# Gate projections inside the attention stages: plain float32 products replaced by split products whose weights are copied between softmax units

## The reference, cut to what matters

```
gates = jax.nn.sigmoid(gate_logits.reshape(B, S, N_BRANCH, D))   # gate_logits = u @ w_in[..., gates]
merged = gates[:, :, 0] * y_mla + gates[:, :, 1] * y_hg + gates[:, :, 2] * y_mem
x = x + merged @ w_out[l]
```

## Time and profile before

| | |
|---|---|
| time, median of 3 runs | 3338.9 us (3335.42 to 3340.44) |
| span of the profiled execution | 3341.3 us |
| TensorE busy | 91% of the span |
| VectorE busy | 48% |
| ScalarE busy | 41% |
| mean granted TensorE clock | 0.947 of full speed |
| bytes read from HBM | 467 MB, 142 GB/s over the span |

### The profile page before, as it was taken

One profiled execution on the slowest core, in us unless ns is written; L12 is line 12 of the kernel. 1 busy time (PEld: TensorE's weight loads), 2 busy tenths in 40 slices (PEclk: granted clock), 3 DMA queues, 4 the chain that ended last, 5 costly groups with the idle time before them and its releaser, 6 DMA issues.

```text
span 3341.3 us, 51733 instructions
## 1 busy us (share of the span) xinstructions
PE 3024.7 (91%) x21202; PEld 2815.0 (84%) x21202; DVE 1608.4 (48%) x2590; ACT 1374.4 (41%) x1959; POOL 6.5 (0%) x10
## 2 busy tenths in 40 slices
PE   5988979899998889999799898999989988899997
PEld 5988768898998778899799886779979988677996
DVE  5556522454555743255555334445555532444555
ACT  4435442243444434243443345534344332553433
POOL 0000000000000000000000000000000000000000
PEclk9999989999999999999899888999989988899998
DMA  5653354565664244366466542346546555224663
GB/s 157 177 156 117 115 139 126 150 179 163 173 167 143 82 126 126 124 170 172 134 181 176 174 115 76 86 130 187 163 144 179 165 149 128 76 77 126 187 169 114
DMA packets 767009, 475.89 MB, mean 142 GB/s; under 512 B 66640, under 2 KB 750192, under 8 KB 766704
## 3 DMA queue, kind: packets, MB, share of 16 engines
q1 hardware_dynamic: 763408, 462.86, 49.0%
q0 software_dynamic: 3424, 10.49, 1.2%
HBM read 467.01 MB, written 6.29 MB: 142 GB/s over the span
## 4 chain that ended last, share of the span: by engine, by line
PE 71%; DVE 11%; DMA 9%; ACT 7%; issue 1%; SPq 0%; DVEq 0%; ACTq 0%
PE ps L740 31%; PE ps L814 31%; PE ps L831 6%; DVE WL L1473 5%; DMA RING<-in_w_ffn_out 4%; ACT WH L1185 3%; DMA RING<-in_w_in 3%; DMA RING<-in_ffn_wo 2%; PE ps L907 2%; DVE U L1447 1%; PE ps L883 1%; PE ps L771 1%; ACT L1182 1%; ACT REGION L1265 0%; DVE U L1455 0%
## 5 line engine op out<-in xcount | busy, mean ns | idle before, releaser
L1185 ACT ACTIVATE WH<-RING 128x2048 fp32r<-128x2048 f32 (+1 forms) x374 | 645.4, 1726 | 1072.0 <-PE ps L814 389.6
L1473 DVE TENSOR_TENSOR WL<-RING,WH 128x2048 fp32r<-128x2048 f32 (+1 forms) x374 | 769.5, 2057 | 617.8 <-ACT WH L1185 617.0
L814 PE MATMUL ps<-UH,WH 128*128 128x256 f32 x2816 | 415.2, 291 | 29.1 <-ACT UH L1203 29.1
L740 PE MATMUL ps<-REGION,RING 128*128 128x256 f32 (+3 forms) x1904 | 396.4, 370 | 29.9 <-DVE REGION L1932 13.1
L831 PE MATMUL ps<-HH,WH 128*128 128x256 f32 x1408 | 400.1, 284 | 19.3 <-DVE WL L1473 19.1
L740 PEld LDWEIGHTS ps<-REGION,RING 128*128 128x128 f32 (+2 forms) x1904 | 338.8, 190 | 86.0 <-DVE REGION L1932 14.8
L814 PE MATMUL ps<-UH,WL 128*128 128x256 f32 x2816 | 403.2, 287 | 8.2 <-DVE WL L1473 8.2
L814 PEld LDWEIGHTS ps<-UH,WH 128*128 128x128 f32 x2816 | 376.5, 196 | 38.7 <-issue 33.1
L814 PE MATMUL ps<-UL,WH 128*128 128x256 f32 x2816 | 401.0, 286 | 0.0
L831 PE MATMUL ps<-HL,WH 128*128 128x256 f32 x1408 | 397.2, 282 | 0.0
L831 PE MATMUL ps<-HH,WL 128*128 128x256 f32 x1408 | 397.0, 282 | 0.0
(11 more groups left out here) (207 smaller groups left out, 2962.6 us busy)
## 6 DMA issues: line engine op xcount, KB each, us to landing
RING<-in_w_ffn_in SPq DMA_DIRECT2D x176, 512.0 KB, 5.0
RING<-in_ffn_wi SPq DMA_DIRECT2D x176, 512.0 KB, 5.0
RING<-in_w_in SPq DMA_DIRECT2D x86, 1024.0 KB, 5.3
RING<-in_w_ffn_out SPq DMA_DIRECT2D x64, 704.0 KB, 4.8
RING<-in_ffn_wo SPq DMA_DIRECT2D x64, 704.0 KB, 4.7
RING<-in_w_out SPq DMA_DIRECT2D x16, 1024.0 KB, 5.2
RING<-in_w_in SPq DMA_DIRECT2D x48, 256.0 KB, 4.6
RING<-in_w_mem_kv SPq DMA_DIRECT2D x8, 1024.0 KB, 5.1
```

The lines of the kernel that those rows point to most:

```text
L740: last = nc.tensor.matmul(o, a, b, start=i == 0, stop=i == len(terms) - 1)
L814: last = nc.tensor.matmul(bank(n, 0, T), a[:, k, side * P:(side + 1) * P], b[:, k, :], start=i == 0 and k == 0, stop=i == 2 and k == DK - 1)
L1185: nc.scalar.activation(part(WH, s), RING[:, s % SLOTS, 0:pl.words[s]], ACT.Copy).then_inc(weights_high, 1)
L1473: v_.tensor_tensor(part(WL, s), RING[:, s % SLOTS, 0:pl.words[s]], part(WH, s).bitcast(FP), ALU.subtract)\
```

## The change

The gate slabs of the five attentions become split slabs. ScalarE and VectorE take them up between units, each at the head of its iteration i, at the slab that `gate_slab` names. TensorE waits for the low part and runs 24 products a tile in place of the plain product.

```diff
@@ def attention(name, kind): in make_plan
-            pl.slab(f[m * ATTN[kind][0] // DK] + m % (DK // ATTN[kind][0]))
+            pl.slab(f[m * ATTN[kind][0] // DK] + m % (DK // ATTN[kind][0]), split=True)
@@ new, beside class Feed
+        def gate_slab(name, kind, i):
+
+            units = ATTN[kind][0]
+            return slab_first[name] + min((i + units // DK) * (DK // units) // 2, 3)
@@ attention, TensorE
-                            wait_weights(pe, sl)
+                            wait_split(pe, sl)
                             product(f[i] + j, [(bank(f[i] + j, 0, T),
-                                                [(slot(sl, DK, 256)[:, k, m % 2 * P:(m % 2 + 1) * P], U[:, k, :]) for k in range(DK)])])
+                                                feature(parts(sl, DK, 256), UP, DK, slice(m % 2 * P, (m % 2 + 1) * P)))])
@@ attention, ScalarE
                     if i < units:
+                        feed.to(gate_slab(name, kind, i))
                         qt = par = i % 2
                         act.wait_ge(max_ready, base + i + 1)
```

## The result

| | before | changed |
|---|---|---|
| time, median of 4 runs on one chip | 3338.7 us (3335.4 to 3340.4) | 3361.7 us (3360.8 to 3368.8) |
| ratio to before | 1 | 1.0072, 95% interval 1.006 to 1.0085 |
| span of the profiled execution | 3341.3 us | 3359.4 us |
| mean granted TensorE clock | 0.947 | 0.938 |

The change costs 23 us, 0.7%; 16.4 were forecast.

A forecast was written before the change was run, and what follows sets the result against it. TensorE, busy 91% of the span, was taken to bound the kernel. Gains of 0.54 us a tile against added loops, starts and clock losses summed to +16.4 us on 3338.9: 3355 us, own range 3346 to 3364, whole range 3334 to 3368.

The forecast's parts named there:

- The clean pair of `A`: Two steady units of A with one slab: 11.25 us against 9.35 before, +1.9 a pair.
- ScalarE's floor: ScalarE's own work in two loaded units: 10.3 us in A, 10.6 in mla, only a little below the loop.
- The starts: Each attention stage's start: slab 0's subtraction delays T(0) by 1.5 us in mla and C, 3.0 A, 2.3 B, 1.9 mem.
- `mem`'s first unit lost its clock: Start of mem: TensorE's idle grows from 2.21 to 4.1 us and slows its clock, +1.9 us for each mem.
- `mla` of 1.0: This stage: slabs 2 and 3, slowed by the bias_rows write, land near 461 and 476; +1.3 us, bounds -18 and +12.
- the rival that gave 3366: In mla of 1.0, slab 2 still lands at 474 and blocks ScalarE in iteration 3: +12 for +1.3; chance 0.12.
- The rival "no change": In mla of 1.0, slabs issued earlier land in time, the 18 us stall goes; about 3336 us; chance 0.12.
- the 16.4 of the sum: All ten attention stages: two A +9.8, two B +3.6, two C and mla of 1.1 +2.7, two mem -1.0, mla of 1.0 +1.3.
- its last sentence: Signs of error: pairs under 9.35 us, a granted clock drop in steady pairs, or the write letting slabs through.
- a loaded pair lasts as long as its loop: Steady units: copy, subtraction, maxima, probabilities, transposes and split tile run in series, closing once in two units; 11.25 us in A.
- the four-pass rule: Gate products: true float32 takes four passes, so three would make a tile 2.62 us; about 3334 us; chance 0.02.
- Faster, as the copies are hidden: Loaded pairs: ScalarE and VectorE make slabs in idle time, a pair of A under 8.4 us; about 3320 us; chance 0.08.

The follow-up runs named there:

- e1: The changed kernel with both ScalarE's copy and VectorE's subtraction of the gate slabs cut to one column (results not right): 3295.8 us, 0.9859 of the kernel before.
- e2: The changed kernel with ScalarE's full copy, but VectorE's subtraction cut to one column: 3328.0 us, 0.9953 of the kernel before.
- the repetition: The changed kernel run once more with no edit: 3362.1 us, 1.0064 of the kernel before.
- e4: The changed kernel with VectorE's subtraction moved behind the probabilities of the unit: 3333.4 us, 0.9973 of the kernel before.
- e11: The changed kernel with 5 and 8 unused filler products ahead of TensorE's two waits in loaded units of mla, A and C: 3346.8 us, 1.0031 of the kernel before.
- e9: The changed kernel with the subtraction moved behind the probabilities and one sigmoid at each stage's end: 3303.3 us, 0.9888 of the kernel before.
- e8: The changed kernel with the write of bias_rows cut into 20 pieces, issued during the following feed-forward block: 3451.2 us, 1.0329 of the kernel before.

## Why the prediction was right where it was, and where it was off

**The mechanism was the one forecast.** TensorE gains 0.54 us a tile (43.3 us over the stages in `e1`), and the copies, queued ahead of their iteration's work, more than take it back through a loop over ScalarE, VectorE and TensorE. The clean pair of `A` was put at 11.25 us and is 11.06, that of `mla` 10.95 and 10.70, that of `B` 18.3 (17.45 + 0.84) and 18.07. ScalarE's floor of 10.3 was seen by itself in `e2` (10.2). The three pairs are 0.2 us below the working and the floor 0.1.

**The starts.** T(0) was put later by 1.5 us in `mla` and `C` (it is 2.3 and 2.0), 3.0 in `A` (2.8 and 2.9), 2.3 in `B` (1.9 and 2.2) and 1.9 in `mem` (1.7). The estimates from the pauses of the earlier trace rows were right in order but for `mla`, where the 0.79 us of cover did not count. `mem`'s first unit lost its clock as foreseen, 2.8 and 2.6 us over the 8.00 of a clean one in the first profile and 1.6 and 1.3 in the repetition, for the 1.9 forecast. The reason given, a wait that grows from 2.21 to about 4.1 us, is not what the runs bear out: the wait did grow, to 3.93, but in `e4` it was 2.13 and both units were slow all the same. The size came out near by luck.

**`mla` of 1.0.** Slabs 2 and 3 were forecast to issue near 433 and 438 and to land near 461 and 476; they issued at 434.1 and 438.75 and landed about 464.7 and 478.1. The forecast had slab 3 alone on the path. Slab 2 blocked ScalarE in iteration 3 as well, for 17.9 us, the mechanism of the rival that gave 3366; but slab 3 landed only 13 us later and two iterations later, so the end of the stage is still slab 3's landing and 20 us, +2.0 for +1.3 (+0.9 in the repetition), and the rival's +12 did not come. The rival "no change" needed the slabs to pass the write; they did not.

**The term that was missing.** Steady units at the low clock, 11.7 us in `A`, `B` and `C`, stand nowhere in the sum. The prediction names them only in its last sentence, as what would make it wrong, and by that sentence it was wrong in this. Without them the stages differ by 16.2 us, against the 16.4 of the sum. That the two agree so well is luck: by stage the rest is off by -1.1 to +0.7 us, and these errors cancel. It is luck, too, that the time lies in the range of 3346 to 3364 us, by 2.3 us at its upper end: the range allowed 8 us for the pairs' length and 4 for `mem`, and nothing for this. So the step "a loaded pair lasts as long as its loop" was right, and the term mis-sized is the clock's: it was counted at 1.9 for each `mem` and at nothing in the pairs, although the loop leaves TensorE idle 2.5 us in each pair of `A`. The rows of before had idle of 2.21 us in `mem` without a slow tile behind it and of 3.52 in `mla` with one; the pauses of a steady pair, 0.83 and 1.62, are each shorter than 2.21 and cost the clock all the same, as `e11` shows by filling them.

**The split rate.** By an estimate from the four-pass rule a tile would have taken 2.62 us. The Trainium skill has it in FP8 and Floating Point Precision, TensorE Precision Notes. The tile took 2.86 to 2.87 against 3.46 for the plain one, 0.83 and not 0.75 of it: the trace does not bear that estimate out at this shape, and the rows were the right choice.

**The rivals.** "Faster, as the copies are hidden" was to decide at a loaded pair under 8.4 us; it is 11.06. Yet the price that this rival gives, 3320, was in reach: `e9` gives the copies time on their engines and reaches 3303, with the sigmoid moved as well.

**Open.** What picks the unit that loses the clock: unit 3 of `A` had 0.69 in one block and 1.00 in the next, at the same pauses, with the same choice again in the repetition and the opposite one in `e8`. And what makes the stretch between the two layers' attentions take 653 us in some executions and 660 in others.

## What to carry to other kernels

Work moved to an engine that is half idle is priced by its place in that engine's queue as much as by its length: close the loop through all engines on paper, find the step that somebody waits for, and put the new work behind it, as here the subtraction behind the probabilities (28 us of the kernel's time for one moved line). A loop that now leaves the tensor engine idle for 2 to 3 us per turn can cost its clock too, so give every such pause a price. A transfer cut into pieces is a different transfer, and its megabytes alone do not price it: here each piece read one partition where the whole read twenty, though that this is the reason was not tested.

## What the runs showed that I had not expected

- Two pauses of 0.83 and 1.62 us inside a steady unit of 11 us were followed by a tile at a granted clock of 0.69, 1.5 us longer than its twin; 13 filler products a pair brought the window back to 1.00, and the filled stages took 5.6 to 7.7 us less.
- Two edits together were worth more than their sum: 32.7 us in the stages (the subtraction's place) and 16.3 (the sigmoid at the end) against 64.6 for both.
- One kernel with no edit between two executions took 652.9 and 660.4 us over the same stretch, at a mean granted clock of 0.97 and 0.95.
- Pieces of 256 KB from one partition took 15 us each and, beside the feed-forward block's loads, brought the engines to 94% busy at 120 GB/s, from 59% at 166 GB/s.
